# The experts' weights of a two-block transformer kernel: split into rounded part and remainder in whole slots of 2048 elements instead of two halves

## The reference, cut to what matters

```python
def swiglu(x, w13, w2):
    a, g = jnp.split(x @ w13, 2, axis=-1)
    return (jax.nn.silu(a) * g) @ w2

def moe_ffn(x, router_w, router_b, w13, w2):
    logits = (x @ router_w).astype(jnp.float32) + router_b.astype(jnp.float32)
    top_v, top_i = lax.top_k(logits, TOP_K)
    wts = jax.nn.softmax(top_v, axis=-1)
    gate = ...
    y = jnp.zeros_like(x)
    for e in range(N_EXPERTS):
        y = y + gate[..., e:e + 1] * swiglu(x, w13[e], w2[e])
    return y
```

## Time and profile before

| What | Value |
|---|---|
| Median of 3 runs | 2346.34 us (2345.07 to 2346.76) |
| Span of the profiled execution, first to last instruction | 2343.8 us |
| Own time of the profiled execution | not given apart from the runs; the median is 2.5 us above the span |
| TensorE busy, of the span | 98% |
| VectorE busy | 74% |
| ScalarE busy | 59% |
| HBM read | 580 MB |

### The profile page before, as it was taken

The page is one execution under the profiler, slowest core; times in us unless marked ns, Lnnn a source line. Parts: engine busy times, 40 slices in busy tenths (PEclk is TensorE's granted clock), DMA queues, the critical chain, the costliest instruction groups (busy, mean ns, idle before and its releaser), DMA issues.

```text
span 2343.8 us, 30911 instructions
## 1 busy us (share of the span) xinstructions
PE 2302.2 (98%) x12538; PEld 1982.3 (85%) x12538; DVE 1734.9 (74%) x2248; ACT 1371.5 (59%) x1793; POOL 71.7 (3%) x91
## 2 busy tenths in 40 slices
PE   9999999999999999999999999999999999999997
PEld 7898888898888999788799888888888888888885
DVE  6756456857555458655555899998999899989997
ACT  4644444544443444444354477777777777777774
POOL 3000001300000000000000000000000000000000
PEclk9999999999999999999999999999999999999998
DMA  8445553626554534555342489999999999999995
GB/s 258 165 162 190 192 192 133 226 74 226 200 186 148 183 124 186 190 181 200 126 140 109 162 350 378 368 362 349 364 374 365 348 367 373 365 357 353 379 364 192
DMA packets 82134, 583.61 MB, mean 249 GB/s; under 512 B 9488, under 2 KB 10816, under 8 KB 12480
## 3 DMA queue, kind: packets, MB, share of 16 engines
q1 hardware_dynamic: 80352, 569.00, 65.2%
q10 hardware_dynamic: 1632, 12.55, 1.9%
HBM read 580.45 MB, written 1.06 MB: 248 GB/s over the span
## 4 chain that ended last, share of the span: by engine, by line
PE 89%; DVE 7%; DMA 2%; ACT 1%; POOL 1%; issue 1%; ACTq 0%; SPq 0%; DVEq 0%
PE bank L452 27%; PE bank L454 27%; PE bank L453 27%; PE bank L449 6%; DVE wl L1467 2%; PE bank L640 2%; DMA raw<-in_ws 2%; PE bank L686 1%; POOL SM L2191 1%; DVE L L1719 1%; DVE X L1566 0%; DVE SM L1499 0%; DVE X L1511 0%; ACT wh L1066 0%; ACT L L1128 0%
## 5 line engine op out<-in xcount | busy, mean ns | idle before, releaser
L1467 DVE TENSOR_TENSOR wl<-raw,wh 128x1024 fp32r<-128x1024 f32 x706 | 829.3, 1222 | 245.6 <-ACT wh L1066 242.8
L1066 ACT ACTIVATE wh<-raw 128x1024 fp32r<-128x1024 f32 x706 | 706.7, 1054 | 347.9 <-PE bank L454 300.9
L452 PE MATMUL bank<-wh,GH 128*128 128x512 f32 x896 | 352.0, 393 | 0.0
L454 PE MATMUL bank<-wh,GL 128*128 128x512 f32 x896 | 349.3, 390 | 0.0
L453 PE MATMUL bank<-wl,GH 128*128 128x512 f32 x896 | 348.9, 389 | 0.0
L1467 DVE TENSOR_TENSOR wl<-spare,wh 128x1024 fp32r<-128x1024 f32 x264 | 309.5, 1220 | 25.8 <-ACT wh L1066 24.5
L1066 ACT ACTIVATE wh<-spare 128x1024 fp32r<-128x1024 f32 x264 | 264.4, 1054 | 63.9 <-PE bank L454 63.8
L452 PE MATMUL bank<-wh,HH 128*128 128x512 f32 (+1 forms) x768 | 289.8, 377 | 10.6 <-DVE HL L1482 6.2
L453 PE MATMUL bank<-wl,HH 128*128 128x512 f32 (+1 forms) x768 | 287.5, 374 | 0.0
L454 PE MATMUL bank<-wh,HL 128*128 128x512 f32 (+1 forms) x768 | 287.2, 374 | 0.0
L452 PE MATMUL bank<-HH,wh 128*128 128x256 f32 x896 | 257.4, 287 | 2.9 <-DVE HL L2029 1.7
(11 more groups left out here) (243 smaller groups left out, 3293.2 us busy)
## 6 DMA issues: line engine op xcount, KB each, us to landing
raw<-in_ws SPq DMA_DIRECT2D x353, 1024.0 KB, 6.2
spare<-in_ws SPq DMA_DIRECT2D x132, 1024.0 KB, 6.9
more<-in_ws SPq DMA_DIRECT2D x48, 1024.0 KB, 4.8
REL<-in_relb ACTq DMA_DIRECT2D x4, 1508.2 KB, 15.4
once<-in_ws SPq DMA_DIRECT2D x4, 1024.0 KB, 11.2
LNB<-in_ln ACTq DMA_DIRECT2D x3, 1024.0 KB, 5.3
LNB<-in_ln ACTq DMA_DIRECT2D x4, 512.0 KB, 4.2
raw<-in_ws SPq DMA_DIRECT2D x2, 816.0 KB, 5.2
```

The costliest lines, as they stand in the source:

```text
L452: T.q.matmul(o, l[0], r[0], start=start, stop=False)
L454: return T.q.matmul(o, l[1], r[0], start=False, stop=stop)
L1066: A.q.activation(sets[c % NSET][0][:, half * i:half * i + half], raws[stream.place[n]][:, half * i:half * i + half], ACT.Copy).then_inc(*h ...
L1467: V.q.tensor_tensor(wl[:, half * i:half * i + half], raw[:, half * i:half * i + half], wh[:, half * i:half * i + half].bitcast(f32), ALU.s ...
```

## The change

Slots from `EXPERTS` on are handled in one piece: one copy of 2048 elements on ScalarE, one subtraction of 2048 on VectorE, one semaphore count each, and TensorE waits for the whole slot before its first matmul. Earlier slots keep their two halves.

```diff
+def pieces(n):
+
+    return 1 if n >= EXPERTS else 2
...
         def t_weights(s, k):
-            T.wait_ge(*lo.at(s, k // stream.half[s]))
+            T.wait_ge(*lo.at(s, min(k // stream.half[s], pieces(s) - 1)))
...
-                half = stream.words[n] // 2
+                half = stream.words[n] // pieces(n)
                 A.wait_ge(landed[stream.place[n]], 16 * stream.turn[n])
                 if c >= NSET:
                     A.wait_ge(*freed[c - NSET])
-                for i in range(2):
+                for i in range(pieces(n)):
                     A.q.activation(sets[c % NSET][0][:, half * i:half * i + half],
                                    raws[stream.place[n]][:, half * i:half * i + half],
                                    ACT.Copy).then_inc(*hi.mark(n, i))
...
-                half = stream.words[n] // 2
+                half = stream.words[n] // pieces(n)
                 wh, wl = sets[c % NSET]
                 raw = raws[stream.place[n]]
-                for i in range(2):
+                for i in range(pieces(n)):
                     V.wait_ge(*hi.at(n, i))
                     V.q.tensor_tensor(wl[:, half * i:half * i + half], raw[:, half * i:half * i + half],
                                       wh[:, half * i:half * i + half].bitcast(f32),
...
                 if stream.split[stream.before[n]]:
-                    S.wait_ge(*lo.at(stream.before[n], 1))
+                    S.wait_ge(*lo.at(stream.before[n], pieces(stream.before[n]) - 1))
```

## The result

The changed kernel takes **2353.37 us** (median of 5 runs, 2353.14 to 2355.08) against 2345.07 us of the kernel before (5 runs, 2344.4 to 2346.76; the three that gave 2346.34 and two more): 8.3 us slower, ratio 1.0036 with a 95% interval of 1.0025 to 1.0048. 2353.6 was predicted. The profiled execution's span grew from 2343.8 to 2351.8 us.

The account below looks back on a forecast made before the run. The prediction took TensorE to bound the experts' stage; 4.5 us at 32 boundaries, 0.3 for SELT, and 1.56 and 0.89 in expert 0 make 7.3, on 2346.3 forecast 2353.6 us, range 2348 to 2359.

Parts of the forecast that it names:

- The bound: Experts' stage: TensorE alone sets the time, so merging pieces can gain nothing while TensorE has no gap.
- The place: Third slot behind chunk boundaries: the third to sixth of seven lie open, 32 waits of 0.14 us, plus two in expert 0.
- The terms of the chain: At a boundary: copy 1.91, handing over 0.04, subtraction 2.28, restart 0.45, together 4.68 us against 4.54 from copy's start today.
- restart to the second matmul: TensorE after a wait: 0.45 us from the end of the subtraction to the start of the slot's second matmul.
- Expert 0: First expert's first two boundaries: TensorE waits 1.56 us at slot 6 and 0.89 us more at slot 10.
- The increment: Whole kernel: 7.3 us slower, from the 32 boundaries, SELT and expert 0; bounds +4.8 to +13.4.
- Absorbed: Rival: the chain fits at the 32 boundaries, only expert 0's 2.4 us stay, 2348.8 us; chance 0.22.
- Loads: Rival: raw buffers released 0.8 us later make loads the bound, 23 us lost, 2369 us; chance 0.06.
- Faster by the saved fixed costs: Rival: 336 slots each save 0.07 us of VectorE's time, 24 us gained, 2322 us; chance 0.04.

Follow-up runs that it names:

- e9: The kernel before, in halves, with ScalarE's SiLU moved ahead of EH and SELT in the experts; 2344.57 us against 2345.78.
- e5: The kernel before, in halves, but loads into an expert's raw buffer wait until the next slot's first half is subtracted too; 2344.72 us against 2345.11.
- e3: The changed kernel, but with halves at the third slot of every chunk, 48 of 336 slots; 2346.18 us against 2345.13 of the kernel before.
- e10: The kernel before, in halves, with three more SiLUs into unused buffers ahead of TT at each boundary of the experts; 2352.41 us against 2345.78.

## Why the prediction was right

- **The bound.** That TensorE alone makes the stage and that nothing can be gained: e9 and e5 show it, and VectorE's and ScalarE's saved time in the changed kernel bought nothing.
- **The place.** The third slot of a chunk, at four boundaries of seven, and at two more of expert 0: all 34 waits stand there, and e3 takes the 32 away by changing the third slots alone.
- **The terms of the chain.** Copy 1.91 predicted, 1.919 measured; subtraction 2.28, 2.290; restart to the second matmul 0.45, 0.45 to 0.46 in 29 of 34 waits and 0.39 in five; the sum 4.68, 4.69. The extrapolation from shorter forms of the same instruction held to half a percent. The Trainium skill (VectorE: DVE Perf Modes, section on the fixed extra latency per instruction) gives 2.291 us for this subtraction, and the trace agrees. What it says of one large tile, that it pays the fixed latency once, holds here as engine time (VectorE's 859 us of busy time from 1382 to 2320 us went down to 831) and not as kernel time.
- **Expert 0.** 1.56 and 0.89 predicted, 1.53 and 0.88 measured. For the first, the restart was 0.39 and not 0.45, half of which the other terms made up. The second wants every link of its chain: VectorE's gates begin only when slot 9 is subtracted, and slot 9's copy waits for a TensorE that is late by the first.
- **What was mis-sized.** The increment: 7.3 predicted, 8.65 in the traces, 8.3 in the medians. The prediction priced a boundary by the time that its second matmul waits, 0.14; that was 0.15. But the matmuls behind a wait come slower too, which it counted nowhere: by the last matmul of the slot a boundary costs 0.185, and the 32 have 5.9 us instead of 4.8.
- **What was luck.** That 2353.6 lies 0.2 us from the measured 2353.37. The forecast started from 2346.3, the median of three runs; with five the kernel before has 2345.07. A base 1.3 too high and an increment 1.0 too low nearly cancel. What the prediction can claim is the mechanism and the increment to 1 us.
- **The rivals.** Absorbed: no, the waits are there. Loads: no, by e5. Faster by the saved fixed costs: no.

## What to carry to other kernels

Before pieces of a hand-over between engines are merged, find the place where the producer starts last relative to its consumer (here behind `EH` and `TT` at a chunk's boundary) and add up the whole chain through it, for whole pieces, against the time that the consumer leaves. An average says nothing: ScalarE was idle for a quarter of the stage, and a chain 0.15 us too long at 32 places, with two longer waits at the start of the stage, cost 0.36% of the kernel. And look for every chain through the instruction that moves: e10's loss stood behind another consumer of the same SiLU.

## What the runs showed of the hardware

Behind a wait TensorE's matmuls come slower for a while. Matmuls of 512 columns start 0.227 us apart in a full row. Behind the longest wait, expert 0's slot 6 in the changed kernel:

```profile
1375.53 0.50 PE L457 MATMUL bank<-wh,GH 128*128 128x512 f32 x1 [1.26 <-DVE wl L1472]
1375.86 0.40 PE L458 MATMUL bank<-wl,GH 128*128 128x512 f32 x1
1376.10 0.40 PE L459 MATMUL bank<-wh,GL 128*128 128x512 f32 x1
1376.33 0.40 PE L457 MATMUL bank<-wh,GH 128*128 128x512 f32 x1
1376.57 0.39 PE L458 MATMUL bank<-wl,GH 128*128 128x512 f32 x1
1376.79 0.39 PE L459 MATMUL bank<-wh,GL 128*128 128x512 f32 x1
```

The second to the fifth start 0.23 to 0.24 apart (0.71 us for the first three steps); the granted clock from 1375 to 1377 us is 1.00, the higher level of 2.4 GHz. It happens behind the 0.15 us waits too (1656.15 to 1656.85 above, 0.70 for three steps), and it is there in the kernel before behind the transposes (0.70 for the same three steps, the mean of slots 16, 20 and 24). Over the ten steps from the second matmul of a slot to its last it comes to 0.03 us more than in a full row, as the mean of the 32 boundaries. This is what makes the slot behind a wait a little late in the table. Why the steps are longer was not tried; it stays open.
